# Unread matmuls ahead of the transposes, and a wait for each chunk of transposed x where there was one for all

## The reference

```python
def first_block(x, ...):                      # two layers
    for l in range(DEPTH):
        h = h + 0.5 * _swiglu(_rmsnorm(h, ffn1_norm[l]), ...)      # ffn1
        h = h + _hybrid_mixer(_rmsnorm(h, mix_norm[l]), ...)       # mix1
        h = h + 0.5 * _swiglu(_rmsnorm(h, ffn2_norm[l]), ...)      # ffn2
    return _rmsnorm(h, final_norm)

def second_block(x, ...):                     # two layers
    h = _layer_norm(x, ln_in_g, ln_in_b)
    for l in range(DEPTH):
        mix = _mixer(h, ...)                                       # mix2
        h = _layer_norm(ALPHA * h + mix, ln1_g[l], ln1_b[l])
        ffn = _peer(h, ...)                                        # peer: 16384 experts
        h = _layer_norm(ALPHA * h + ffn, ln2_g[l], ln2_b[l])
    return h
```

## Time and profile before

| | |
|---|---|
| median of 3 runs | 3269.84 us (3257.9 to 3272.41) |
| the profiled execution: its own time | 3269.65 us |
| its span, first to last instruction | 3267.9 us |
| mean granted TensorE clock | 0.964 of full speed |
| PE busy | 3055.3 us, 93% |
| DVE, ACT, POOL busy | 2134.5 us (65%), 1535.3 us (47%), 409.5 us (13%) |
| share of the chain that ended last | PE 78%, DVE 7%, POOL 6%, issue 6%, ACT 3% |

### The profile page before, as it was taken

How to read it: one execution, slowest core, us unless ns; L and a number is a source line. 1 busy time by engine, 2 the same in 40 slices (tenths; PEclk the granted TensorE clock), 3 DMA queues, 4 the chain that set the end, 5 groups by cost and what they waited for, 6 DMA issues and landing times.

```text
span 3267.9 us, 58680 instructions
## 1 busy us (share of the span) xinstructions
PE 3055.3 (93%) x20820; PEld 2800.7 (86%) x20820; DVE 2134.5 (65%) x3718; ACT 1535.3 (47%) x2356; POOL 409.5 (13%) x235
## 2 busy tenths in 40 slices
PE   7999989999899997789999999998879999999997
PEld 7988879899888897679999988887769999988886
DVE  4546555555564555657978767776657977867776
ACT  4445444444544444435555545554535555545553
POOL 0000100000010000206830000000105840000000
PEclk9989999999899998889999999999989999999999
DMA  6543235555322554346766677775336775677774
GB/s 198 185 134 117 79 132 185 164 174 186 116 97 82 168 183 145 114 141 191 227 202 182 182 231 241 241 241 186 127 131 186 228 211 181 185 229 241 241 241 167
DMA packets 213007, 579.57 MB, mean 177 GB/s; under 512 B 23728, under 2 KB 88528, under 8 KB 212352
## 3 DMA queue, kind: packets, MB, share of 16 engines
q1 hardware_dynamic: 209216, 562.62, 54.4%
q0 software_dynamic: 3648, 14.99, 1.3%
HBM read 541.34 MB, written 36.18 MB: 177 GB/s over the span
## 4 chain that ended last, share of the span: by engine, by line
PE 78%; DVE 7%; POOL 6%; issue 6%; ACT 3%; DMA 0%; POOLq 0%; SPq 0%; DVEq 0%; ACTq 0%
PE work L649 34%; PE acc L672 32%; POOL wsp L629 6%; PE acc L755 3%; PE acc L1162 3%; PE work L725 2%; DVE xsp L1598 1%; DVE wsp L416 1%; PE work L885 1%; ACT wsp L413 1%; PE work L1002 1%; PE work L766 1%; DVE h L1629 0%; DVE h L1960 0%; DVE h L1954 0%
## 5 line engine op out<-in xcount | busy, mean ns | idle before, releaser
L649 PE MATMUL work<-xsp,wsp 128*128 128x256 f32 x12096 | 1518.3, 286 | 24.5 <-DVE scratch L1787 9.2
L649 PEld LDWEIGHTS work<-xsp,wsp 128*128 128x128 f32 x12096 | 1487.9, 194 | 36.3 <-issue 18.2
L416 DVE TENSOR_TENSOR wsp<-ring,wsp 128x1024 fp32r<-128x1024 f32 x824 | 1010.9, 1228 | 691.0 <-ACT wsp L413 690.8
L413 ACT ACTIVATE wsp<-ring 128x1024 fp32r<-128x1024 f32 x944 | 993.8, 1053 | 635.1 <-PE work L649 265.4
L672 PE MATMUL acc<-wsp,hsp 128*128 128x512 f32 x4128 | 955.5, 391 | 9.2 <-issue 9.2
L672 PEld LDWEIGHTS acc<-wsp,hsp 128*128 128x128 f32 x4128 | 771.8, 188 | 166.7 <-issue 9.5
L629 POOL TENSOR_TENSOR wsp<-ring,wsp 128x1024 fp32r<-128x1024 f32 x120 | 303.6, 2542 | 169.3 <-ACT wsp L413 168.9
L1539 ACT ACTIVATE hsp<-arena 128x256 fp32r (+1 forms) x256 | 107.2, 419 | 355.6 <-PE acc L672 336.1
L537 POOL TENSOR_TENSOR st<-st,mhalf 128x2 f32<-128x2 f32 x12 | 13.3, 1106 | 1664.8 <-DVE st L1613 858.3
L2165 DVE TENSOR_TENSOR one_hots<-iota,selT 128x512 bf16<-128x512 bf16 x256 | 97.2, 422 | 81.8 <-PE acc L1162 81.7
L2203 DVE TENSOR_TENSOR hsp<-arena,hsp 128x256 fp32r<-128x256 f32 x256 | 109.0, 426 | 57.0 <-ACT hsp L1539 57.0
(11 more groups left out here) (312 smaller groups left out, 1919.3 us busy)
## 6 DMA issues: line engine op xcount, KB each, us to landing
ring<-in_stream SPq DMA_DIRECT2D x944, 512.0 KB, 3.6
back<-acts_dram SPq DMA_DIRECT2D x252, 128.0 KB, 3.6
acts_dram<-acts SPq DMA_DIRECT2D x128, 128.0 KB, 3.6
acts_dram<-arena SPq DMA_DIRECT2D x124, 128.0 KB, 4.3
rows_sb<-in_rows POOLq DMA_DIRECT2D x10, 512.0 KB, 5.0
h_saved_dram<-h POOLq DMA_DIRECT2D x2, 1024.0 KB, 4.2
h<-h_saved_dram POOLq DMA_DIRECT2D x2, 1024.0 KB, 6.5
scratch<-in_levels POOLq DMA_DIRECT2D x3, 448.0 KB, 4.6
```

The source lines that it names most:

```text
L413: self.eng.activation(dst[:, 0, :], src, ACT.Copy).then_inc(high_done, 1)
L416: self.eng.tensor_tensor(dst[:, 1, :], src, dst[:, 0, :].bitcast(F32), ALU.subtract)\
L649: mm = pe.matmul(out_, lhsT=w[:, a, 128 * c:128 * c + 128], rhs=xsp[:, b, c, :], start=(c == 0 and n == 0), stop=(c == DC - 1 and n == 2))
```

## The change

TensorE's program alone is changed. `busy_bank` issues n matmuls of 512 columns on operands that lie in `xsp` already, into a bank of `work` that the transposes later overwrite; nobody reads the result. `make_xT` calls it ahead of the wait for the norm: 26 times in `mix1` and in every `ffn` but the first, 65 and 45 times in `mix2` of layers 0 and 1, 45 times in `peer`; 11 more stand ahead of `V`. Where `make_xT` waited for its last four banks at its end, it now returns its group, and the first product waits for a chunk just ahead of the first matmul that reads it.

```diff
+            def busy_bank(G, q, n):
+                G.claim(pe, q)
+                for _ in range(n):
+                    pe.matmul(G.bank(q)[:, :], lhsT=xsp[:, 0, 6, 0:128],
+                              rhs=xsp[:, 0, 4:6, :].rearrange("p c t -> p (c t)"), start=True, stop=True)
-            def product_unit(G, i, out_, it=0):
+            def product_unit(G, i, out_, it=0, x=None):
                 w = G.unit(pe, i, it)
                 for c in range(DC):
+                    if x is not None and c >= 4:
+                        x.freed(pe, c)
...
-            def make_xT(part, src, name, count, first=0, n=DC):
+            def make_xT(part, src, name, count, first=0, n=DC, busy=0):
                 G = Group(part, name)
+                busy_bank(G, 3, busy)
                 for q in range(n):
...
-                for q in range(n - 4, n):
-                    G.freed(pe, q)
+                return G
...
             def ffn(part, n, tiles):
-                make_xT(part, xs, "xT", ("xs_ready", n))
+                X = make_xT(part, xs, "xT", ("xs_ready", n), busy=26 if n > 1 else 0)
...
             def out_projection(part, n):
                 for c in range(DC):
+                    if c >= 4:
+                        X.freed(pe, c)
                     down_unit(G, c, xsp[:, :, c, :], c == 0, c == DC - 1)
...
+                X = make_xT(part, xs, "xT", ("xs_ready", 3 * l + 2), busy=26)
...
-                make_xT(part, y, "yT0", ("half_y", l + 1), 0, 4)
+                Y0 = make_xT(part, y, "yT0", ("half_y", l + 1), 0, 4)
...
                 for c in range(4):
+                    Y1.freed(pe, c)
                     down_unit(G, c, xsp[:, :, 4 + c, :], False, c == 3)
...
+                X = make_xT(part, h, "xT", ("ln_ready", 2 * l + 1), busy=45 if l else 65)
...
+                X = make_xT(part, h, "xT", ("ln_ready", 2 * l + 2), busy=45)
...
+                G = Group(part, "V")
+                busy_bank(G, 0, 11)
                 pe.wait_ge(g_moved, GROUPS * (l + 1))
-                G = Group(part, "V")
```

More of the change, by code:

```diff
@@ L684, in gate_up @@
                         G.claim(pe, 2 * t + m, it)
-                        product_unit(G, i + m, G.bank(2 * t + m)[:, 0:T], 6 * it)
+                        product_unit(G, i + m, G.bank(2 * t + m)[:, 0:T], 6 * it, X if t == 0 and m == 0 else None)
                 def down(t, first, last, it=0):
@@ L707, in out_projection @@
             def out_projection(part, n):
-                make_xT(part, y, "yT", ("y_ready", n))
+                X = make_xT(part, y, "yT", ("y_ready", n))
                 G = Group(part, "wout")
@@ L730, in mix1 @@
             def mix1(part, l):
-                make_xT(part, xs, "xT", ("xs_ready", 3 * l + 2))
+                X = make_xT(part, xs, "xT", ("xs_ready", 3 * l + 2), busy=26)
                 pe.wait_ge(const_in, 48)
@@ L764, in mix1 @@
                     for c in range(DC):
+                        if b == 0 and c >= 4:
+                            X.freed(pe, c)
                         for m, (px, pw) in enumerate(PARTS):
@@ L1031, in mix1 @@
                 for c in range(4):
+                    Y0.freed(pe, c)
                     down_unit(G, c, xsp[:, :, c, :], c == 0, False)
-                make_xT(part, y, "yT1", ("y_ready", l + 1), 4, 4)
+                Y1 = make_xT(part, y, "yT1", ("y_ready", l + 1), 4, 4)
                 G = Group(part, "wout1")
                 for c in range(4):
+                    Y1.freed(pe, c)
                     down_unit(G, c, xsp[:, :, 4 + c, :], False, c == 3)
             def mix2(part, l):
-                make_xT(part, h, "xT", ("ln_ready", 2 * l + 1))
+                X = make_xT(part, h, "xT", ("ln_ready", 2 * l + 1), busy=45 if l else 65)
                 G = Group(part, "small")
@@ L1111, in peer @@
             def peer(part, l):
-                make_xT(part, h, "xT", ("ln_ready", 2 * l + 2))
+                X = make_xT(part, h, "xT", ("ln_ready", 2 * l + 2), busy=45)
                 G = Group(part, "tt")
@@ L1115, in peer @@
                     G.claim(pe, q)
-                    product_unit(G, q, G.bank(q)[:, 0:T])
+                    product_unit(G, q, G.bank(q)[:, 0:T], x=None if q else X)
                 for q in range(12, 16):
```

## The result

| | before | after |
|---|---|---|
| median of 6 runs each, us | 3271.12 (3257.9 to 3276.49) | 3243.23 (3239.3 to 3247.1) |
| ratio to before, 95% interval | | 0.9918 (0.9901 to 0.9935) |
| profiled execution, us (span) | 3269.65 (3267.9) | 3247.1 (3245.3) |
| mean granted clock | 0.964 | 0.978 |
| time within the span with the granted clock at half speed, us | 235.1 | 140.7 |

The changed kernel is 0.8% faster and lands on the forecast of 3243.

The account below looks back on a forecast made before the run. TensorE holds 78% of the chain of waits; seams cost norm, half-speed transposes and products, and the last chunk's wait. Seven terms sum to 26.7 us: 3269.65 - 26.7 = 3243 us; bounds 3233 to 3254, 8-in-10 range 3228 to 3261.

Parts of the forecast that it names:

- heads of ffn: Three ffn heads: product 3.3 us after the transposes, not 5.07, plus 1.9 from one half-speed product; 7.2 us saved.
- heads of peer: Two peer heads: from transposes to product 3.3 us instead of 4.81, 1.5 each; 3.0 us saved.
- heads of mix1: Two mix1 heads: 0.5 each from DVE's earlier start and pace, 1.0 each from the gates' clock; 3.0 us saved.
- tails of mix1: Two layers: head products and `wout1` each start 1.25 us sooner, needing only chunk 0; 5.0 us saved, bounds 3 and 8.
- heads of mix2: Two mix2 heads: 0.3 each from the earlier start, 1.4 from the small product's matmuls; 2.0 us saved.
- `yT` of mix2: Two layers, no filler: `wout` starts 1.55 us sooner each, the clock's earlier return 0.85 each; 4.8 us saved.
- V: Ahead of V, two seams: filler keeps the second seam's clock up; 1.7 us saved, bounds 0 and 3.5.
- The filler at nothing: Ahead of every head's norm: unread matmuls, 0.228 us each, stay hidden with 0.45 to 0.7 us to spare; cost 0.
- the third rival: Every head: unread matmuls take more than 0.228 us, so the filler outruns the norm; about 3305 us, chance 0.04.
- The first rival: Seven ffn, peer and mix1 seams: clock falls late, in the product, about 2.5 us lost each; 3270 us, chance 0.10.
- the terms of order: Gains left without the clock's: ffn 4.0, peer 2.5, tail 5.0, yT 3.1; 14.6 us.
- The second and third rival: Second: filler doesn't hold the clock, or DVE's chains in the mixers eat its gains; 3254 us, chance 0.17.

Follow-up runs that it names:

- The 39: Changed kernel with 39 instead of 26 unread matmuls at the five heads of ffn and mix1; 3258.40 us, 0.9958 of before.
- the experiment with SyncE's order: Changed kernel with SyncE's loads of the token blocks that V reads put ahead of the weight load; 3234.53 us, 0.9908 of before.
- the last kernel of the experiments: Changed kernel with the first product of ffn and peer waiting again for all four last banks; 3243.40 us, 0.9919 of before.

## Why the prediction was right, and where it was right by luck

The terms, from the two profiled executions:

| term | forecast, us | measured, us |
|---|---|---|
| heads of ffn | 7.2 | 7.8 |
| heads of peer | 3.0 | 4.3 |
| heads of mix1 | 3.0 | 0.2 |
| tails of mix1 | 5.0 | 8.0 |
| heads of mix2 | 2.0 | 3.2 |
| `yT` of mix2 | 4.8 | 5.3 |
| V | 1.7 | -1.5 |
| sum | 26.7 | 27.3 |
| not forecast: start and first product | 0 | 1.7 |
| not forecast: middle of mix1, of mix2 | 0 | -1.8, -4.6 |
| total | 26.7 | 22.6 |

- *The filler at nothing.* Right: 26 in 6.05 us, 65 in 14.89, 45 in 10.36, 11 in 2.68, all but the last ending 0.5 us or so before their norm. It is 0.233 a matmul, where 0.228 was taken and 0.245 was the point from which the third rival decides. The 39 priced that rival.
- *The heads of ffn and peer.* Right in mechanism; a product at 3.06 and 2.72 where 3.3 was taken. Of the ffn's 7.8, 1.9 is the one product that had run partly at half speed (13.63 in the earlier trace rows, 11.78 now), as forecast.
- *The heads of mix1.* This step failed in its size. 1.0 each was taken from the clock, on the idea that the gates would profit from a start at full speed. From transposes to gates went as forecast (5.09 and 5.05 to 4.53), but the fall comes under the gates and lasts 10.2 us as before; the gates took 7.97 and 8.79 before, 8.88 and 8.76 now. The bounds, -1.5 to 2.7 each, hold it. The price of half speed was also read too low: a stretch counts the matmuls that reach over its edges, so 2.0/11 = 0.18 is less than the pace. By the earlier trace rows 24 of the 48 ran at 0.108, and (7.97 - 24 x 0.108)/24 = 0.22 is left for the others; in the trace of before their starts lie 0.213 us apart. All slow, the 48 take 48 x 0.213 = 10.2 us, which makes the lower bound -2.3. The same reading gave 0.39 for a 512-column matmul, whose starts lie 0.43 apart there at half speed; the third rival would have cost more than it says.
- *The tails.* The upper bound came true, since the head products were quicker besides: 24 in 4.54 us, where the earlier trace rows have 5.46. The clock falls later there and is up again sooner.
- *V.* This step failed outright: its bounds were 0 and 3.5, and it lost 1.5. From the end of the last U product to the end of V, layer 0 gained 0.5 us (356.1 to 355.5) and layer 1 lost 1.9 (353.3 to 355.2). The prediction asked what becomes of the idle time, but not what is late next. The token block behind a weight load was, and the experiment with SyncE's order shows it.
- *The middles.* Nothing was changed there, and I let them stand at nothing. In layer 1 before, the clock happened to be 1.00 under `mix2`'s token groups; timeline of before:

```profile
2314.38 11.16 PE L725 MATMUL work<-wsp,xsp 128*128 128x512 f32 x48 [2.00 <-DVE scratch L2004]
```

In the profile after they run partly at half speed, behind a wait of the same length:

```profile
1305.15 12.78 PE L736 MATMUL work<-wsp,xsp 128*128 128x512 f32 x48 [2.00 <-DVE scratch L2022]
```

  This row is of layer 0; in layer 1 the clock falls once a group as well (2292.2, 2309.3, 2326.4). The 4.6 us that the middle of `mix2` took back are all in layer 1. Nothing says that they are a price of the change: the last kernel of the experiments, with the same instructions there, needs 101.7 us for this stage in layer 1, the changed kernel 106.7.
- *The first rival* had 0.10. It did not come true in this kernel. The filler-only kernel shows its mechanism, a fall that comes late and in the product, but in two ffn heads and the two `wout1` at some 1.5 us each, not in seven seams at 2.5; that its 3269 is near the rival's 3270 is chance, since the terms of order, which the rival keeps, are missing there. The prediction's argument against it was the `yT1` row, 1.80 us of wait and a clock of 1.00 behind it. The filler-only kernel has 1.91 at that place and falls. The conclusion held, the argument did not: a single row at full speed did not show that such a gap is safe.
- *The second and third rival* did not come true: the clock is 1.00 under the filler in all nine heads, and each of them has a wait of 0.46 to 0.79 us left behind it.

So the total is right, but over errors of both signs, of up to 4.6 us, and the range of 3228 to 3261 was needed more than the 3243 shows.

## What to carry to other kernels

Unread work that keeps TensorE's clock up gave nothing here by itself (0.9992, against 0.9918 with the shorter waits), and in part the profile shows why: falls moved from idle time into a product. So look at the short waits behind the filler and cut them too. Not every one of them costs a fall: the heads' 1.22 us alone did not. Give the filler a bank that nothing in the seam has to free, and a length that ends ahead of what it bridges: an overrun cost its length (2.3 us a head here), and a bank that was not free turned a gain of 15 us in `mix2` into one of 1. And when a stall goes, look along the queue of whatever the freed stage reads next: here a load issued behind another took back what V had won.

## What the runs showed of the hardware

- The granted clock can fall to 0.50 while TensorE is busy without a pause: under the 16-column matmuls of the gates it fell in the stretch 223 to 225 and stayed at 0.50 in 225 to 227, each with 2.00 us of 2.00 busy.
- Two waits of nearly one length can end differently. Behind 1.80 us `wout1` ran 48 matmuls in 11.16 us, behind 1.91 in 12.76. In both kernels the clock had been low under the head products and was back at 1.00 some 11 us ahead of the wait. The two waits of 2.00 us in `mix2`, 11.16 against 12.78, and the one ffn head of three that kept its clock, say the same, and so do the waits of 2.97 and 2.08 us behind the transposes as filler. What decides between them the runs don't settle.
- Transposes of f32 against an identity hold the clock at 1.00, 46 of them in 5.18 us, 80 in 8.89; a wait of 2.08 us behind the 80 let it fall.
- This kernel's spread, 20 us over 21 runs of before, has its like in the stages without a change: the middle of `mix1` (from its transposes to those of `yT0`) took from 181.2 to 188.8 us in profiled executions of kernels whose instructions there are the same. A gain of under 7 us in that stage can't be read from one profile of each.
